# The second norm's factor moved behind the up product of a 128-partition float32 network

## What is computed

```python
x = x + rms_norm(merged @ w_out[l], post_mix_g[l])
hf = rms_norm(x, pre_ffn_g[l])
u = jnp.square(jax.nn.relu(hf @ w_up[l])) @ w_down[l]
x = x + rms_norm(u, post_ffn_g[l])
```

## Time and profile before

| what | value |
|---|---|
| median of 3 executions | 2353.8 us (2353.13 to 2356.7) |
| the profiled execution: its time, its span | 2353.59 us, 2351.8 us |
| TensorE matmul busy | 2198.1 us, 93% of the span |
| TensorE weight load busy | 1769.4 us, 75% |
| VectorE, ScalarE, GpSimd busy | 1029.8, 815.2, 830.6 us |
| mean granted TensorE clock | 0.951 of full |

### The profile page before, as it was taken

The page is one execution under the profiler, slowest core; times in us unless marked ns, Lnnn a source line. Parts: engine busy times, 40 slices in busy tenths (PEclk is TensorE's granted clock), DMA queues, the critical chain, the costliest instruction groups (busy, mean ns, idle before and its releaser), DMA issues.

```text
span 2351.8 us, 29721 instructions
## 1 busy us (share of the span) xinstructions
PE 2198.1 (93%) x12420; PEld 1769.4 (75%) x12428; DVE 1029.8 (44%) x1650; ACT 815.2 (35%) x1242; POOL 830.6 (35%) x367
## 2 busy tenths in 40 slices
PE   5999889899799999999998899999999989999997
PEld 4767678888678888867776678888877467888886
DVE  3023884545532012237326754442248556444323
ACT  3344422134333133223334354443233334444322
POOL 3423210014434444453322244444443125444442
PEclk9999987799889999999999999999999889999998
DMA  5322100004213323322211123323312112323321
GB/s 216 104 81 85 54 29 2 2 28 143 81 54 99 99 90 99 98 72 63 63 50 50 52 65 99 99 91 107 97 56 90 36 37 73 97 90 106 100 90 63
DMA packets 52861, 182.97 MB, mean 78 GB/s; under 512 B 5608, under 2 KB 5616, under 8 KB 52600
## 3 DMA queue, kind: packets, MB, share of 16 engines
q1 hardware_dynamic: 52728, 181.08, 23.8%
HBM read 176.32 MB, written 7.62 MB: 78 GB/s over the span
## 4 chain that ended last, share of the span: by engine, by line
PE 84%; DVE 11%; ACT 2%; DMA 1%; issue 1%; POOL 1%; SPq 0%; DVEq 0%; ACTq 0%
PE ps L319 19%; PE ps L320 19%; PE ps L321 19%; PE ps L1430 3%; PE ps L2384 2%; PE ps L339 1%; PE ps L345 1%; PE ps L2386 1%; PE ps L2385 1%; PE ps L340 1%; PE ps L432 1%; PE ps L1000 1%; PE ps L2920 1%; PE ps L438 1%; DVE work L1556 1%
## 5 line engine op out<-in xcount | busy, mean ns | idle before, releaser
L178 POOL TENSOR_TENSOR split_units<-raw_units,split_units 128x1024 fp32r<-128x1024 f32 x314 | 762.6, 2438 | 1447.1 <-ACT split_units L169 1447.1
L319 PE MATMUL ps<-x_split,split_units 128*128 128x512 f32 x1296 | 512.6, 396 | 10.4 <-POOL split_units L178 9.6
L320 PE MATMUL ps<-x_split,split_units 128*128 128x512 f32 x1296 | 508.4, 392 | 0.0
L321 PE MATMUL ps<-x_split,split_units 128*128 128x512 f32 x1296 | 507.9, 392 | 0.0
L169 ACT ACTIVATE split_units<-raw_units 128x1024 fp32r<-128x1024 f32 x314 | 329.6, 1052 | 400.3 <-PE ps L321 355.3
L319 PEld LDWEIGHTS ps<-x_split,split_units 128*128 128x128 f32 x1296 | 245.7, 190 | 68.0 <-POOL split_units L178 11.5
L320 PEld LDWEIGHTS ps<-x_split,split_units 128*128 128x128 f32 x1296 | 245.6, 189 | 52.4 <-issue 1.7
L321 PEld LDWEIGHTS ps<-x_split,split_units 128*128 128x128 f32 x1296 | 245.6, 190 | 51.8
L319 PE MATMUL ps<-hidden_split,split_units 128*128 128x512 f32 x608 | 237.3, 390 | 0.0
L321 PE MATMUL ps<-hidden_split,split_units 128*128 128x512 f32 x608 | 236.6, 389 | 0.0
L320 PE MATMUL ps<-hidden_split,split_units 128*128 128x512 f32 x608 | 236.5, 389 | 0.0
(11 more groups left out here) (411 smaller groups left out, 3205.3 us busy)
## 6 DMA issues: line engine op xcount, KB each, us to landing
raw_units<-stream SPq DMA_DIRECT2D x314, 512.0 KB, 3.5
bias_rows<-bias_line SPq DMA_DIRECT2D x1, 2816.0 KB
gate_rows<-work SPq DMA_DIRECT2D x10, 256.0 KB, 2.1
work<-gate_rows SPq DMA_DIRECT2D x10, 256.0 KB, 2.8
x<-x_t SPq DMA_DIRECT2D x4, 512.0 KB, 5.2
work<-bias_rows SPq DMA_DIRECT2D x1, 2048.0 KB
out_t<-x SPq DMA_DIRECT2D x8, 256.0 KB
vec<-vectors SPq DMA_DIRECT2D x1, 1163.5 KB, 10.7
```

What stands on the lines that cost most here:

```text
L178: gpsimd.tensor_tensor(self.split[:, u % SPLIT, 1, :], self.raw[:, u % RING, :], self.split[:, u % SPLIT, 0, :].bitcast(F32), ALU.subtract ...
L319: TE.matmul(out, high, rhs(0, k), start=(k == 0), stop=False)
L320: TE.matmul(out, high, rhs(1, k), start=False, stop=False)
L321: ins = TE.matmul(out, low, rhs(0, k), start=False, stop=last and shift is None)
```

## The change

In `post_mix_pre_ffn`, the second norm's factor is no longer needed before the product. ScalarE writes the high part of x times gain as soon as x's tile is added (`Identity` with the gain as scale) and squares the tile after it; VectorE makes the low part in the same loop that scales and adds. GpSimd has nothing left in the norm. The squares are added by VectorE after the norm loop (seven adds), TensorE sums them over partitions in the middle of tile 3 (at k = 6), ScalarE takes the root, VectorE the reciprocal, TensorE spreads the factor into bank 6 after tile 3, and VectorE copies it into a tile of SBUF. Each bank of `up_a` and `up_b` is then read by VectorE (maximum with zero, times factor), ScalarE squares the result and rounds it, VectorE subtracts. ScalarE rounds the unit of tile 3 ahead of its wait for the sums of squares. `layer_norm` reads the mean's sums from PSUM once more in place of squaring the mean out of `col`, and spreads the mean into bank 4.

```diff
@@ product @@
-                split_product(pe, bank(m % 4), n_k, rhs, tile_ready, m + 1)
+                split_product(pe, bank(m % 4), n_k, rhs, tile_ready, m + 1, late if m == AT_FIRST else None)
@@ post_mix_pre_ffn @@
-            def pe(p):
-                squares_after_linear(p)
-                p.wait_ge(norm_act.sem, norm_act.at(1 + KD))
-                p.wait_ge(norm_pool.sem, norm_pool.at(1))
-                factor_pe(p, (w[:, SUM, :], w[:, SQS + KD - 2, :], w[:, SQS + KD - 1, :]), dve_n=KD + 3)
             def act(a):
                 root_after_linear(a, RMS_EPS, 1)
                 for t in range(KD):
                     a.wait_ge(norm_dve.sem, norm_dve.at(t + 3))
-                    S.activation(w[:, SQS + t, :], xt(t), ACT.Square).then_inc(norm_act.sem, 1)
-                factor_act(a, 4, RMS_EPS)
-                scale_act(a, TMP, KD + 3)
+                    S.activation(xs[:, 0, t, :], xt(t), ACT.Identity, scale=v("pre_ffn_g", t)).then_inc(norm_high.sem, 1)
+                    S.activation(w[:, FFN_SQUARES + t, :], xt(t), ACT.Square).then_inc(norm_act.sem, 1)
             def dve(d):
                 mean_square_dve(d)
                 d.wait_ge(norm_pe.sem, norm_pe.at(3))
-                in_pairs(d, scaled, added)
-                factor_dve(d, KD + 2)
-                scale_dve(d, "pre_ffn_g", TMP, 5)
-            def pool(p):
...
+                marks = []
+                for t in range(KD + 2):
+                    if t < KD:
+                        marks.append(dve_chain.mark(scaled(t)))
+                    if 1 <= t <= KD:
+                        d.wait_ge(dve_chain.sem, marks[t - 1])
+                        added(t - 1)
+                    if t >= 2:
+                        d.wait_ge(norm_high.sem, norm_high.at(t - 1))
+                        V.scalar_tensor_tensor(xs[:, 1, t - 2, :], xt(t - 2), v("pre_ffn_g", t - 2),
+                                               xs[:, 0, t - 2, :].bitcast(F32), ALU.mult, ALU.subtract
+                                               ).then_inc(norm_low.sem, 1)
@@ layer_norm @@
-                spread_columns(p, MEAN, 0)
+                spread_columns(p, SPREAD_MEAN, 0)
...
-                dve_chain.link(d, V.tensor_tensor(var, mean, mean, ALU.mult))
+                dve_chain.link(d, V.scalar_tensor_tensor(var, bank(MEAN, 4, 4), -1.0 / D, mean, ALU.mult, ALU.mult))
@@ stage_relu2_up @@
+            def factor_sums(pe, k):
+                if k == LATE:
+                    pe.wait_ge(side_dve.sem, side_dve.at(1))
+                    for i in range(NT):
+                        ins = TE.matmul(bank(SUMS, i, 1), w[:, FFN_SQUARES, tok(0, i)], one, start=True, stop=True)
+                    ins.then_inc(side_pe.sem, 1)
+                def factor_spread(p, m):
+                    if m == AT_FIRST:
+                        p.wait_ge(side_dve.sem, side_dve.at(2))
+                        for i in range(NT):
+                            ins = TE.matmul(bank(MEAN, i * P, P), col[:, 8 + i:9 + i].to_broadcast([P, P]), ident,
+                                            start=True, stop=True)
+                        ins.then_inc(side_pe.sem, 1)
...
                     wts.round_high(act, S, u0 + SPLIT)
                     before.act(act)
+                    wts.round_high(act, S, u0 + 1 + SPLIT)
+                    act.wait_ge(side_pe.sem, side_pe.at(1))
+                    S.activation(col[:, 8:12], bank(SUMS, 0, 4), ACT.Sqrt, scale=1.0 / D,
+                                 bias=eps_of[RMS_EPS]).then_inc(side_act.sem, 1)
                 for m in range(n_tiles):
                     wts.round_high(act, S, u0 + m + SPLIT)
-                    act.wait_ge(tile_ready.sem, tile_ready.at(m + 1))
+                    act.wait_ge(tile_read.sem, tile_read.at(m + 1))
                     if m >= 2:
-                        act.wait_ge(dve_out.sem, dve_out.at(m - 1))
-                    S.activation(w[:, RL + m % 2, :], bank(m % 4), ACT.Relu).then_inc(read_act.sem, 1)
-                    high(m)
+                        act.wait_ge(low_out.sem, low_out.at(m - 1))
+                    S.activation(w[:, SQ + m % 2, :], w[:, RL + m % 2, :], ACT.Square).then_inc(act_out.sem, 1)
+                    act.wait_ge(act_out.sem, act_out.at(m + 1))
+                    S.activation(hidden1[:, 0, m, :], w[:, SQ + m % 2, :], ACT.Copy).then_inc(high_out.sem, 1)
...
+                    for t in range(1, KD):
+                        dve.wait_ge(norm_act.sem, norm_act.at(t + 2))
+                        ins = V.tensor_tensor(w[:, FFN_SQUARES, :], w[:, FFN_SQUARES, :], w[:, FFN_SQUARES + t, :],
+                                              ALU.add)
+                        if t < KD - 1:
+                            dve_chain.link(dve, ins)
+                    ins.then_inc(side_dve.sem, 1)
+                    dve.wait_ge(side_act.sem, side_act.at(1))
+                    V.reciprocal(col[:, 8:12], col[:, 8:12]).then_inc(side_dve.sem, 1)
+                    dve.wait_ge(side_pe.sem, side_pe.at(2))
+                    dve_chain.link(dve, V.tensor_copy(factor, bank(MEAN)))
                 for m in range(n_tiles):
                     r, q = w[:, RL + m % 2, :], w[:, SQ + m % 2, :]
-                    dve.wait_ge(read_act.sem, read_act.at(m + 1))
-                    V.tensor_tensor(q, r, r, ALU.mult).then_inc(dve_out.sem, 1)
+                    dve.wait_ge(tile_ready.sem, tile_ready.at(m + 1))
+                    V.scalar_tensor_tensor(r, bank(m % 4), 0.0, factor, ALU.max, ALU.mult).then_inc(tile_read.sem, 1)
```

More of the change, by code:

```diff
@@ L364, in first_products, with product @@
                 ins.then_inc(tile_ready.sem, 1)
-        def product(pe, n_tiles, n_k, rhs, read, before=None, beside=None, prior=None):
+        def product(pe, n_tiles, n_k, rhs, read, before=None, beside=None, prior=None, late=None):
             if before is not None:
@@ L597, in dve @@
                 d.wait_ge(norm_pe.sem, norm_pe.at(3))
-                in_pairs(d, scaled, added)
-                factor_dve(d, KD + 2)
-                scale_dve(d, "pre_ffn_g", TMP, 5)
-            def pool(p):
[L603 to L613, removed]
+                marks = []
[10 more added lines that the diff above has]
+                                               ).then_inc(norm_low.sem, 1)
+            return Before(pe=squares_after_linear, act=act, dve=dve, pool=nothing, high=high_scaled,
+                          ready=lambda p, t: p.wait_ge(norm_low.sem, norm_low.at(t + 1)),
+                          counts=((norm_pe, 3), (norm_act, KD + 1), (norm_dve, KD + 2), (norm_high, KD),
+                                  (norm_low, KD)))
         def post_ffn():
@@ L676, in centred @@
                         d.wait_ge(norm_pe.sem, norm_pe.at(4))
-                    return V.tensor_tensor(xt(t), xt(t), bank(MEAN), ALU.add)
+                    return V.tensor_tensor(xt(t), xt(t), bank(SPREAD_MEAN), ALU.add)
                 def scaled(t):
@@ L2029, in stage_relu2_up @@
             u0 = wts.block // UNIT
+            factor = w[:, FFN_FACTOR, :]
+            LATE = KD - 2
+            def factor_sums(pe, k):
[4 more added lines that the diff above has]
+                    ins.then_inc(side_pe.sem, 1)
             @block.tensor
             def _(pe):
-                product(pe, n_tiles, KD, of(xs), read_act, before, prior=prior)
+                def factor_spread(p, m):
[5 more added lines that the diff above has]
+                        ins.then_inc(side_pe.sem, 1)
+                if before is None:
+                    product(pe, n_tiles, KD, of(xs), tile_read, prior=prior)
+                else:
+                    product(pe, n_tiles, KD, of(xs), tile_read, before, factor_spread, late=factor_sums)
             weight_programs(block, act=False, before=before)
@@ L2065, in stage_relu2_up @@
             tile_ready.close(n_tiles)
-            read_act.close(n_tiles)
-            dve_out.close(n_tiles)
+            tile_read.close(n_tiles)
+            act_out.close(n_tiles)
             high_out.close(n_tiles)
             if before is not None:
+                side_pe.close(2)
+                side_act.close(1)
+                side_dve.close(2)
                 before.close()
@@ L2993, in network @@
             ("up_a", lambda: stage_relu2_up(post_mix_pre_ffn())),
-            ("down_a", lambda: stage_linear(FF1 // 2, of(hidden1), "copy", wt(36), prior=read_act)),
+            ("down_a", lambda: stage_linear(FF1 // 2, of(hidden1), "copy", wt(36))),
             ("up_b", lambda: stage_relu2_up(prior=tile_read)),
-            ("down_b", lambda: stage_linear(FF1 // 2, of(hidden1), "add", wt(36), sums="squares", prior=read_act)),
+            ("down_b", lambda: stage_linear(FF1 // 2, of(hidden1), "add", wt(36), sums="squares")),
             ("even_in", stage_even_in),
```

7 lines of the change are left out of this document (2 added, 5 removed).

## The result

The changed kernel takes 2338.1 us (median of 4, 2337.9 to 2341.0), the one before beside it 2353.7: ratio 0.9934, interval 0.9917 to 0.9951, so 15.5 us less (11.5 to 19.5). The forecast was 2341, 12.7 less. The profiled execution took 2338.0 with a span of 2336.2, against 2353.59 and 2351.8. In the rows PE, DVE, ACT and POOL are TensorE, VectorE, ScalarE and GpSimd, PEld is the loading of weights, and a bracket at a row's end gives how long the engine stood idle before it and what released it.

What follows compares the result with a forecast made beforehand. TensorE holds 84% of the chain, so only its idle or slow time can be won, chiefly a 13.7 us wait for the second norm's squares. 10.2 + 2.5 = 12.7 us off 2353.6 gives 2341; range 2335 to 2349.

Steps and rivals of the forecast that it cites:

- rival C: Kinder clock: products start at full level, tile 4 restarts with half the low stretch or none; 2337 us, chance 0.12.
- The start: Ahead of up_a: TensorE starts at 636.5, with the second norm's sums, root, reciprocal, spread and scaling off the path.
- The supply of x: Norm loop: VectorE's third operation takes 0.75 us, 1.93 us a tile; TensorE, once behind at low level, is never short.
- Rival B: Norm loop: VectorE's third operation is slow (1.73 us), 2.95 us a tile, and TensorE waits; 2346.5 us, chance 0.17.
- The three tiles: Up_a's first three tiles, 72 matmuls: the first 12 at low clock level, 5.1 us; the last 12 end at 655.2.
- Tile 3: Up_a: TensorE's pause before tile 3 is 1.05 us where it was 2.9, clock kept, VectorE's seven adds hidden.
- The round trip: Before up_a's tile 4: 9.1 us pause, its unit queued in ScalarE's list behind the factor; then a low restart, 2.4 us.
- The up stretch in all: Start of up_a's tile 4, at full level: 675.4 where it was 685.56, a gain of 10.2 us.
- The layer norms: Two of four norms: mean's square 0.16 us instead of 1.98, factor spreads 1.04 and 1.45 us earlier, 2.5 us.
- D: From the first product to the end of tile 4, TensorE stays at the low level; up to 2360 us, chance 0.05.
- E: The wait only moves: the pause before tile 4 is 22 us rather than 9; 2351 us, chance 0.04.

Runs made afterwards that it cites:

- the experiment with the adds: The changed kernel with all seven adds of squares on GpSimd beside the norm loop, VectorE's seven adds removed: 0.9943, median 2341.5 us.
- the kernel with the units ahead: The changed kernel with ScalarE rounding the units of tiles 4 and 5 ahead of its wait for the sums of squares: 0.9914, median 2334.3 us.
- this part alone: The kernel before with all of the change but the layer norms' part: 0.9952, median 2343.3 us.
- fillers: Five float32 matmuls nobody reads, in TensorE's pauses ahead of up_a: 2333.1 us against 2324.1 without them; on the changed kernel alone 0.9927, median 2336.4.
- the edit of the maximum: The changed kernel with the layer norms' maximum with zero given a second operand in PSUM: 0.9930, median 2335.5 us.
- both edits: The changed kernel with units of tiles 4 and 5 rounded ahead, sums at k = 2, spread at k = 5, and the maximum's PSUM operand: 0.9878, median 2324.1 us.
- the last of the study: The kernel with all edits and five unread matmuls, but sums asked for at k = 6 and the spread at k = 7 of tile 3: 0.9896, median 2327.7 us.
- all edits with fillers: The kernel with units ahead, earlier factor and the maximum's PSUM operand, plus five unread matmuls ahead of up_a: 0.9914, median 2333.1 us.

## Why the prediction was right, and where it was off

The time fell inside the stated range, and the order of events in the up stretch came as forecast. It lies 0.4 us below the narrower band of the forecast itself (2338.5 to 2344.5) and nearer to rival C's 2337, so the total alone does not tell the forecast from C; the traces do.

**The start.** Forecast: TensorE at 636.5, which in this execution's time is 635.56. Measured 635.56.

**The supply of x.** Forecast: 0.75 us for VectorE's third operation and 1.93 us a tile. Measured 0.742 and 1.92. Rival B's form of trouble exists, but only with GpSimd at work, as the experiment with the adds shows.

**The three tiles.** Forecast: 12 matmuls at the low level. Measured 9 in 3.9 us, then full; the clock was kinder by 0.6 us.

**Tile 3.** The pause was 0.94 us (forecast 1.05) and the clock kept its level; the last add, held by the unit of tile 3, ended at 655.49, 3.7 us before the sums at 659.21, where the sum without the hold had about 6. By the rule that the prediction took from the Trainium skill (SBUF — State Buffer, SBUF: two separate sides), that GpSimd and a VectorE instruction with two SBUF inputs exclude each other for a whole instruction, it was to be 3.7; the trace agrees: the last add lasted 2.78 us, from 652.70, beside GpSimd's unit of 652.57 to 654.94.

**The round trip.** Forecast: 9.1 us of pause, by ScalarE's list. Measured 9.07, and the kernel with the units ahead shows the cause: the pause goes, and what is left of it is the wait for the bank. The restart was low for 12 matmuls (to 676.88), as taken.

**The up stretch in all.** Forecast 10.2; measured 10.9 between units 51 and 66, and 11.3 (8.5 to 14.4) with this part alone.

**The layer norms.** Here a term was mis-sized, twice and in opposite directions, and the near hit of the total owes something to luck. The forecast of 2.5 us took everything behind the mean's square to be 1.8 us earlier until TensorE's spread of the mean decides. Measured: the distance from GpSimd's unit to the factor's spread went from 3.55 us to 2.96 (1716.82 to 1719.78), 0.6 in each of two norms, 1.2 in all, because the hold moved three instructions on, to the maximum with zero. The prediction asked what is late next on TensorE and not what else on VectorE has its operands in SBUF alone. Against that stands what the forecast left out, the level of TensorE's clock behind the norms: 1.5 us behind the second (22 matmuls in 7 us before, 28 after) and 1.0 between units 240 and 246. With it the norms brought 3.3 us (1.4 to 5.4) alone and 3.8 by the unit starts. So the terms that the forecast had come to 10.9 + 1.2 = 12.1 us, close to its 12.7; most of the step from there to 15.5 is a clock gain of 2.5 us that no term of it held, and another 0.5 lay ahead of the change (unit 51).

The rivals C and D fell in their form: the products did start at the low level, and it came back after 3.9 us. C was right that the clock could be kinder, but it put this in the up stretch. B's slow operation and E's longer pause did not come.

## What to carry to other kernels

Where a factor is moved behind a product, look at what stands behind the wait for it in each engine's list: here nearly half of the 20 us won at the start was lost because ScalarE held the next weight unit back. When an instruction is freed from a lock that another engine holds, the next one with the same kind of operands takes its place; follow the chain until the lock is released. An engine that is made faster starts its neighbours earlier: fillers that brought TensorE's level back sooner cost 9 us, at least 5 of them because GpSimd's units met VectorE's adds while TensorE was already waiting for these. And compare stretches between the same two instructions of two traces where medians differ by less than single executions do: the edit of the maximum is worth 4 us and the medians could not tell it.

## What the runs showed of the hardware

- A VectorE `tensor_scalar` of four columns from SBUF to SBUF took 1.03 us, until the end of a GpSimd instruction of 2.35 us; as an instruction with one operand in PSUM it took 0.16 us beside it.
- While GpSimd ran three instructions of 2.4 us and more in a row (8.24 us), VectorE's adds with two SBUF inputs (0.69 us alone) came through once per GpSimd instruction: three in 8.27 us.
- An edit that brought two spreads of the second layer norm 0.6 us closer together went with 28 instead of 22 matmuls in the 7 us from the first product on, in ten traces with it against two without. At the third norm the same edit left the level low.
- Single executions differ before any edit takes effect: the start of unit 51 lies between 577.54 and 582.84 us in the twelve traces, whose programs are the same up to there. In the stretch from 500.0 to 577.5 us the granted clock was 1.00 in three of the four earliest (the changed kernel, the one with both edits, and the last of the study) and 0.96 in the two latest (the maximum's edit, and all edits with fillers).
